# Stick-breaking attention with queries on partitions: sigmoid, product scan and transposed weights in place of matmul sums of log terms

## The reference

```python
z = jnp.einsum('bqhd,bkhd->bhqk', qb, kf) * (B_DH ** -0.5)
valid = k_pos[None, :] < qpb[:, None]
log_keep = jnp.where(valid, jax.nn.log_sigmoid(-z), 0.0)
after = lax.cumsum(log_keep, axis=3, reverse=True) - log_keep
a = jnp.where(valid, jnp.exp(jax.nn.log_sigmoid(z) + after), 0.0)
return jnp.einsum('bhqk,bkhd->bqhd', a, vf)
```

## Time and profile before

| | |
|---|---|
| time of three runs | 1991.29 us median, 1987.05 to 1993.68 |
| profiled execution, first to last instruction | 1986.7 us (0.35 us below the shortest of the three times) |
| TensorE busy, share of the span | 1859.7 us, 94% |
| VectorE | 1151.5 us, 58% |
| ScalarE | 1031.0 us, 52% |
| GpSimd | 387.6 us, 20% |
| mean granted clock of TensorE | 0.975 |
| second attention, from the first scores on | 1002.4 to 1744.8 us |
| `mix_b`, gate units of 384 rows | 1839.2 to 1923.0 us |

### The profile page before, as it was taken

One profiled execution on the slowest core, in us unless ns is written; L12 is line 12 of the kernel. 1 busy time (PEld: TensorE's weight loads), 2 busy tenths in 40 slices (PEclk: granted clock), 3 DMA queues, 4 the chain that ended last, 5 costly groups with the idle time before them and its releaser, 6 DMA issues. The chain is left out here.

```text
span 1986.7 us, 31724 instructions
## 1 busy us (share of the span) xinstructions
PE 1859.7 (94%) x11429; PEld 1615.1 (81%) x11429; DVE 1151.5 (58%) x2317; ACT 1031.0 (52%) x2452; POOL 387.6 (20%) x597
## 2 busy tenths in 40 slices
PE   4999999999999899999699999999999999899996
PEld 3888878888788779999587888888888888689995
DVE  5456465574555642355257667676767575844545
ACT  5355454564545532354256656575757575822345
POOL 0132231322313100156101010111111111200441
PEclk7999999999999999999799999999999999999999
DMA  4121112211122143221110202111112021242113
GB/s 155 45 79 38 49 49 60 65 39 49 49 60 65 44 152 90 65 73 59 60 39 22 65 28 70 38 50 39 55 33 60 28 60 49 77 135 90 54 54 127
DMA packets 161803, 125.07 MB, mean 63 GB/s; under 512 B 10992, under 2 KB 152624, under 8 KB 161648
## 3 DMA queue, kind: packets, MB, share of 16 engines
q1 hardware_dynamic: 160784, 122.85, 20.2%
q10 hardware_dynamic: 864, 0.20, 0.1%
HBM read 89.49 MB, written 33.52 MB: 62 GB/s over the span
## 5 line engine op out<-in xcount | busy, mean ns | idle before, releaser
L107 PE MATMUL pj<-h_high,area 128*128 128x384 f32 (+1 forms) x1536 | 380.4, 333 | 18.2 <-issue 5.8
L107 PE MATMUL pj<-area,h_high 128*128 128x384 f32 (+1 forms) x1152 | 333.0, 352 | 6.3 <-issue 5.5
L107 PEld LDWEIGHTS pj<-h_high,area 128*128 128x128 f32 x1536 | 271.0, 192 | 23.7 <-issue 11.1
L107 PE MATMUL pj<-h_low,area 128*128 128x384 f32 (+1 forms) x768 | 251.7, 328 | 0.0
L107 PEld LDWEIGHTS pj<-area,h_high 128*128 128x128 f32 (+1 forms) x1152 | 204.0, 181 | 18.6 <-issue 5.5
L1208 ACT ACTIVATE lb_m<-lb_sc 128x512 f32<-128x512 f32 (+4 forms) x200 | 88.5, 486 | 227.1 <-PE lb_sc L1642 196.3
L107 PE MATMUL pj<-area,h_low 128*128 128x384 f32 (+1 forms) x576 | 195.3, 339 | 0.0
L1557 POOL TENSOR_TENSOR lb_o<-lb_o,lb_keep 128x512 f32<-128x512 f32 (+3 forms) x80 | 77.6, 970 | 572.5 <-ACT lb_keep L1237 565.9
L1396 DVE SCALAR_TENSOR_TENSOR lb_s<-lb_sc,lb_m 128x512 f32<-128x512 f32 (+4 forms) x200 | 109.9, 549 | 69.0 <-ACT lb_m L1218 69.0
L107 PEld LDWEIGHTS pj<-h_low,area 128*128 128x128 f32 x768 | 147.6, 192 | 0.0
L455 ACT ACTIVATE la_p<-la_sc,la_nm 128x128 f32<-128x128 f32 (+5 forms) x144 | 105.8, 737 | 33.8 <-DVE la_nm L652 32.9
(11 more groups left out here) (310 smaller groups left out, 4394.2 us busy)
## 6 DMA issues: line engine op xcount, KB each, us to landing
stage<-in_a_w_in SPq DMA_DIRECT2D x60, 192.0 KB, 3.2
stage<-in_b_w_in SPq DMA_DIRECT2D x60, 192.0 KB, 3.2
stage<-in_ple_w_gate SPq DMA_DIRECT2D x22, 512.0 KB, 3.8
h_low<-o_t SPq DMA_DIRECT2D x14, 528.0 KB, 6.4
mix_b_xs<-x_mid SPq DMA_DIRECT2D x8, 528.0 KB
lift_xt<-in_x SPq DMA_DIRECT2D x8, 512.0 KB, 4.6
stage<-in_a_w_in SPq DMA_DIRECT2D x16, 256.0 KB, 5.0
out_ak<-la_tok SPq DMA_DIRECT2D x8, 512.0 KB, 3.3
```

The costliest lines, as they stand in the source:

```text
L107: last = pe.matmul(out, x, y, start=start and n == 0, stop=stop and n == 2, **kw)
```

## The change

`stick_layer` is turned round: queries are on partitions and keys in the free dimension. A pair is now a tile of 128 queries with up to 512 keys; tiles 4 to 7 have two pairs, the later keys first. ScalarE computes sigmoid(-z) into `remain` and sigmoid(z) into `a`, both from PSUM. VectorE turns `remain` into the running product by a scan that goes backwards over the keys, and for the earlier keys starts from the later pair's last value. GpSimd multiplies `a` by the product shifted by one key (VectorE does so for the sample). TensorE transposes the weights in blocks of 128 keys into `flip`, ScalarE copies them to `wt`, and TensorE multiplies them with the values once per 256 queries, accumulating over all key blocks in PSUM, so that the scaling by `keep` and the additions into `o` are gone. Scores banks shrink from four to three, `flip` takes two. The gate uses the sigmoid directly. `stick_layer` names the table set `sigmoid_and_others` before its first group. `diff_layer` and `mix_phase` are the same text; their lines are lower by 67 in `mix_phase`.

```diff
...
-    PAIRS = [(0, b) for b in range(4)] + [(1, 0), (2, 0)] + [(1, b) for b in range(1, 8)]
-    UNITS = [(c, b, hd) for c, b in PAIRS for hd in range(1 if c == 2 else 2)]
-    NP, N, SPLIT = len(PAIRS), len(UNITS), len(UNITS) - 1
...
+    SAMPLE_Q = NT
+    PAIRS = [(q, 0) for q in range(4)] + [(SAMPLE_Q, 0)] + [(q, c) for q in range(4, NT) for c in (1, 0)]
+    UNITS = [(q, c, hd) for q, c in PAIRS for hd in range(1 if q == SAMPLE_Q else 2)]
+    BANKS = [(0, 1), (2, 0), (1, 2), (0, 1), (1, 2)] + [(0, 1), (2, 0), (1, 2)] * 2 + [(0, 1), (2, 0)]
+    FIRST_KEY = [0, 512, 0, 512, 0] + [512, 0] * 4
+    VALUES = [0, 1, SAMPLE_Q, 2, 3]
+    NP, N = len(PAIRS), len(UNITS)
+    SAMPLE = PAIRS.index((SAMPLE_Q, 0))
+    HQ = 2 * P
...
+    value_pair = lambda v: SAMPLE if v == SAMPLE_Q else PAIRS.index((2 * v + 1, 0))
+    value_nth = lambda v: VALUES.index(v) + 1
+    VALUES_AT = {value_pair(v) + 2: v for v in VALUES}
+    width = lambda i: PAST + DEC if i == SAMPLE else min(QC, (PAIRS[i][0] + 1) * P - PAIRS[i][1] * QC)
+    diagonal = lambda i: i != SAMPLE and PAIRS[i][1] == PAIRS[i][0] // 4
+    carried = lambda i: i > SAMPLE and PAIRS[i][1] == 0
+    keys_end = lambda i: FIRST_KEY[i] + width(i) + carried(i)
...
+        remain = [sb(f"remain{i}", [P, 2 * QC]) for i in range(2)]
+        a_ = [sb(f"a{i}", [P, PAST + DEC]) for i in range(4)]
+        wt, wt_sample = [sb(f"wt{i}", [P, NT, HQ]) for i in range(2)], sb("wt_sample", [P, SB, 2 * DEC])
...
+        flip, acc, sc = pb("flip", [P, 2, 512]), pb("acc", [P, 512]), pb("sc", [P, 3, 512])
...
+                def keep(s):
                     act.wait_ge(S["z"], at.next("z"))
...
+                    act.activation(remain_of(s), scores_of(s), ACT.Sigmoid, scale=-1.0).then_inc(S["keep"], 1)
...
+                def sigmoid(s):
+
+                    act.wait_ge(S["w_turned"], at.nth("w_turned", s - 3) if s >= 4 else at.before("w_turned"))
+                    act.activation(weights_of(s), scores_of(s), ACT.Sigmoid).then_inc(S["sig"], 1)
+
+                def move(s):
+                    i, hd = pair(s), UNITS[s][2]
+                    q, c = PAIRS[i]
+                    act.wait_ge(S["w_turned"], at.nth("w_turned", s + 1))
...
+                    act.wait_ge(S["pv"], at.nth("pv", value_nth(q // 2 - 1)) if q >= 2 else at.before("pv"))
+                    nb = width(i) // P
+                    act.activation(wt[hd][:, 4 * c:4 * c + nb, q % 2 * P:(q % 2 + 1) * P],
+                                   flip[:, hd, 0:width(i)].rearrange("p (b n) -> p b n", n=P), ACT.Copy).then_inc(S["moved"], 1)
...
                 for i in range(NP + 1):
                     if i < NP:
                         for s in units(i):
-                            size(s)
-                        for s in units(i):
-                            exp(s)
-                        for s in units(i):
-                            log(s)
+                            keep(s)
+                            sigmoid(s)
                     if i >= 1:
                         for s in units(i - 1):
-                            weights(s)
-                        if PAIRS[i - 1][1] > 0:
-                            keep(i - 1)
+                            move(s)
                     if i - 1 in GATE_AT:
-                        gate_log(GATE_AT[i - 1])
-                    if i - 2 in GATE_AT:
-                        gate_sigmoid(GATE_AT[i - 2])
+                        gate_sigmoid(GATE_AT[i - 1])
...
+            act.preload_act_table_set("sigmoid_and_others")
...
+                def scan(s):
+                    i, hd = pair(s), UNITS[s][2]
+                    dve.wait_ge(S["keep"], at.next("keep"))
+                    x, first = remain_of(s)[:, ::-1], 1.0
+                    if carried(i):
+                        dve.wait_ge(S["scan"], at.nth("scan", s - 1))
+                        first = remain[hd][:, QC:QC + 1]
+                    dve.tensor_tensor_scan(out=x, data0=x, data1=x, initial=first, op0=ALU.mult, op1=ALU.min).then_inc(S["scan"], 1)
+
...
+                def take(v):
+                    dve.wait_ge(S["pv"], at.nth("pv", value_nth(v)))
...
+                    out, c = slice(v * HQ, (v + 1) * HQ), v // 2
+                    if v % 2 == 0:
...
-                add(NP - 1)
-                finish(1)
+                take(VALUES[-1])
+                dve.wait_ge(S["taken"], at.all("taken"))
...
+                def product(s):
+                    pool.wait_ge(S["scan"], at.nth("scan", s + 1))
+                    pool.wait_ge(S["sig"], at.nth("sig", s + 1))
+                    after = after_of(s)
+                    out = weights_of(s)[:, 0:after.shape[1]]
+                    pool.tensor_tensor(out, out, after, ALU.mult).then_inc(S["a"], 1)
...
+                            last = pe.matmul(scores_of(s), qt[x][f, q * P:(q + 1) * P],
+                                             kt[y][f, par, c * QC:c * QC + width(i)], start=n == 0 and not diagonal(i),
...
+                def turn_weights(i):
+                    for s in units(i):
+                        hd = UNITS[s][2]
+                        if i == SAMPLE:
+                            pe.wait_ge(S["a_sample"], at.all("a_sample"))
+                        else:
+                            pe.wait_ge(S["a"], at.nth("a", a_nth(s + 1)))
+                        pe.wait_ge(S["moved"], at.nth("moved", copied(s)) if copied(s) else at.before("moved"))
+                        x = weights_of(s)
+                        n = 2 * DEC if i == SAMPLE else P
+                        for b in range(0, width(i), P):
+                            rows = min(P, width(i) - b)
+                            last = pe.transpose(flip[0:rows, hd, b // P * n:(b // P + 1) * n], x[:, b:b + rows], ident[0:n, 0:n])
+                        last.then_inc(S["w_turned"], 1)
+
+                def values(v):
+                    i = value_pair(v)
...
+                    blocks = SB if v == SAMPLE_Q else 2 * v + 2
...
+                                q = P if b == 2 * v + 1 else 0
+                                last = pe.matmul(acc[f, q:HQ], tok_v[:, par, b, f], wt[hd][:, b, q:HQ], **kw)
...
-                    if i >= 2:
-                        values(i - 2)
+                    if i in VALUES_AT:
+                        values(VALUES_AT[i])
                     if i >= 1:
-                        for s in units(i - 1):
-                            after(s)
-                        if PAIRS[i - 1][1] > 0:
-                            column_sums(i - 1)
+                        turn_weights(i - 1)
                     if i in (0, 2, 3):
                         turn(at, i + 5)
...
-                values(NP - 1)
+                values(VALUES[-1])
...```

The places in the order of instructions that differ. First TensorE in a middle step of a group, whose pair has 512 columns (`lb_sc` scores, `lb_s` log terms, `lb_acc` values, `pj` projection). Before:

```order
L1642 MATMUL lb_sc<-lb_qk_high 128x512 x2
L1642 MATMUL lb_sc<-lb_qk_high,lb_qk_low 128x512 x2
L1642 MATMUL lb_sc<-lb_qk_low,lb_qk_high 128x512 x2
L1709 MATMUL lb_acc<-lb_a,lb_tok 64x512 x2
L1672 MATMUL lb_sc<-lb_s_high,lb_tri 128x512
L1672 MATMUL lb_sc<-lb_s_low,lb_tri 128x512
L1672 MATMUL lb_sc<-lb_s_high,lb_tri 128x512
L1672 MATMUL lb_sc<-lb_s_low,lb_tri 128x512
L1683 MATMUL lb_third<-lb_s_high,lb_half 128x512
L1683 MATMUL lb_third<-lb_s_low,lb_half 128x512
L1683 MATMUL lb_third<-lb_s_high,lb_half 128x512
L1683 MATMUL lb_third<-lb_s_low,lb_half 128x512
```

More of the change, by code:

```diff
@@ L1044, in stick_layer @@
-                     z=N, size=N, exp=N, log=N, soft=N, high=SPLIT, low=SPLIT, after=N, a=N, sums=CARRIED,
-                     keep=CARRIED, scaled=CARRIED, added=NP - 1, sampled=1, pv=NP, dve_link=4, o_ready=3,
-                     pe_tick=0, fill=1, pads=1)
+                     tok_stored=64, g_ready=3, g_normed=3, g_sig=3, g_done=3, qs_ready=1,
+                     z=N, keep=N, sig=N, scan=N, a=N - 1, a_sample=1, w_turned=N, moved=N, pv=len(VALUES), taken=len(VALUES), dve_link=0,
+                     o_ready=3, fill=1, pads=1)
@@ L1448, in finish @@
+                    ins = dve.tensor_tensor(o[:, out], acc[:, 0:HQ], gate[:, out], ALU.mult)
+                    ins.then_inc(S["taken"], 1)
                 def finish(c):
@@ L1633, in scores @@
-                        for hd in range(2):
-                            last = pe.matmul(slot[:, hd, PB * DEC:], unit[:, :], hide[:, 0:DEC], **masked)
+                        first = BANKS[i][0]
+                        for n, (x, y) in enumerate(((0, 0), (1, 0), (0, 1))):
+                            pe.matmul(sc[0:2 * DEC, first, :], qs[x][:, :], kpt[y][:, :], start=n == 0, stop=n == 2,
+                                      skip_group_check=True)
+                        new = sc[0:2 * DEC, first + 1, 0:DEC]
@@ L1635, in scores @@
+                        pe.matmul(new, hide_sample[:, :], unit[:, 0:DEC], start=True, stop=False, skip_group_check=True)
```

(23 more changed lines are left out.)

424 lines of the change are left out of this document (150 added, 274 removed).

## The result

| | before | the change |
|---|---|---|
| median | 1991.26 us | 1957.76 us |
| range, four runs each | 1987.05 to 1993.68 | 1955.77 to 1959.91 |
| profiled span | 1986.7 | 1954.0 |
| TensorE busy | 1859.7 | 1780.0 |
| VectorE, ScalarE, GpSimd busy | 1151.5, 1031.0, 387.6 | 1023.8, 976.7, 548.1 |

A forecast was written before the change was run, and what follows sets the result against it. TensorE was taken to bound the second attention, busy 721.2 of 742.4 us. The sum 1986.7 - 98 + 1 + 55 = 1944.7 us of span, with the median 4.6 above, gave 1949 us; 8 in 10 range 1922 to 1990.

The forecast's parts named there:

- the two large terms: Second attention about 97 us shorter (-98 of TensorE work, +1 of waits); table loads in mix_b +55 us.
- The work term: Second attention, TensorE: 7.5 us added, 18.5 removed, 1.3 saved by reshaping; net -12.3 a group, -98 in eight.
- with 0.10 for entering, as above, one is 0.08: Second attention: TensorE's price per 128x128 transpose, from four taking 0.42 us; 7.5 us a group in all.
- The wait term: Second attention: new waits for weights 20 us, against 19.3 going; net +1, bounds -10 and +35.
- second rival: Attention: GpSimd's product takes 1.8, not 1.30 us, slowed by VectorE's passes; 15 to 35 us more, 1964 to 1984; chance 0.15.
- hand-overs: Second attention: included in the 20 us of waits, beside about 8 us in half-piece steps and some 8 in the last group.
- None becomes the bound by volume: Second attention: ScalarE and VectorE have room; GpSimd's product comes to about 25 us a group of some 80.
- dearer switch: Rival in mix_b: a table switch costs more than its 1.28 us row; at 2.56, 2028 us, slower; chance 0.13.
- the ring: mix_b gates: units and weight splits in series over ScalarE and VectorE; 62 loads lie on it, first-pass visit 12.8 us.
- then the split up to the next unit's Exp 3.35: mix_b, first gate pass: last part of a visit's 12.8 us, read from 1950.20 to 1953.55; seven visits +16.
- The hidden loads: Third rival, mix_b: the loads stay hidden since TensorE had ScalarE idle in 51 of 83.8 us; 1894 to 1910; chance 0.05.
- The chain: Second rival, attention: scores to transposable weights, through ScalarE, VectorE and GpSimd in series, becomes the bound; 1964 to 1984; chance 0.15.

The follow-up runs named there:

- turned_twice: set_back with every transpose of weights issued twice: 1941.78 us, 45.8 us above set_back.
- head1_vector: set_back with head 1's product of weights and scan moved from GpSimd to VectorE: 1883.11 us, 12.8 below set_back.
- both_vector: set_back with both heads' products on VectorE instead of GpSimd: 1890.92 us, 5.0 below set_back.
- set_back: The changed kernel with natural_log_exp_and_others named at the start of mix_b's ScalarE stream, leaving one load there: 1895.94 us, 0.953 of before.
- before_switch: The kernel before with sigmoid_and_others named at the start of mix_b's ScalarE stream, so the same 67 loads appear: 2053.24 us, 1.031 of before.
- add_later: The changed kernel, loads kept; in mix_b GpSimd's sum for a unit waits until that unit's clamp is done: 1953.81 us, 0.981 of before.

## Why the prediction was right, point by point

**The sum.** 1949 was predicted and 1957.76 measured, 8.8 us more, on the side and inside the range. By the finer rows above, the two large terms came out as -90.0 (forecast -97) and +62.0 (forecast +55): both mechanisms as described, both sizes 7 us too kind. The 4.7 us that came back, 2.8 before the attention and 1.9 in the outputs, are no merit of the forecast: the code there is the same.

**Attention.** A middle group lasts 82.05 us (the same matmul of past keys stands at 1417.29 and 1499.34). Before, five of seven last 93.5 and two 95.0; each of the two has a short stretch at the lower clock (a mean of 0.66 from 1197 to 1202 us and 0.67 from 1571 to 1576), which no middle group has now. Like against like that is 11.4 less. The forecast had 12.3 of work and, with the earlier trace rows's 1.9 us a group gone and 1 come, some 0.9 of waits.

The work term was 0.9 too large. Counted on TensorE from start to start, the 77 transposes of this group take 8.9 us where the forecast had 7.5, and the projections 0.5 more than before; against that, the sums and the sample gave 19.5 and not 18.5. The step that was off for the transposes is "with 0.10 for entering, as above, one is 0.08": four of them still take 0.41 to the next instruction, as in the earlier trace rows, but the eight shown take 0.93 and not 0.74, and turned_twice has 0.10 each. The wait term was mis-sized as well: the group keeps 1.8 us on TensorE, as many as before, since GpSimd's product takes 1.67 and not 1.30. That was the second rival's mechanism at three quarters of its size (it took 1.8), and its claim "the two may slow each other" holds: whichever starts second pays (last section).

The waits for weights come to 22.6 us on TensorE, where the text had 20 with hand-overs. The 36.6 of the weight loads overstates the price, as head1_vector and both_vector show. "None becomes the bound by volume" held, with GpSimd's products at 33 us a group and not 25. So for a middle group the forecast was 1.8 us too kind. Part of that was made up by things that it didn't know: the first group gave 15.6, of which 2.5 are waits that only that group had, and the two slow stretches of before gave 3. That is luck.

The last group is only 3.0 us shorter than before (1581.41 to 1652.1 against 1671.20 to 1744.9), with 9.7 us of waits for products. Behind such waits the granted clock fell, too; no run here takes the waits out of this group alone, so that they caused it isn't shown. After:

```profile
1613.40:1619.40 6.00, 5.98 (x22) 4.80 (x23) 4.46 (x6) 4.01 (x8) 2.81 (x3) 0.50 0.64 262
...
1640.00:1650.40 10.40, 8.62 (x35) 5.96 (x35) 3.17 (x3) 3.15 (x6) 4.05 (x2) 0.51 0.00 0
```

At 0.50 TensorE runs at 1.2 GHz; ahead of the first row stand two waits of 1.90 and 1.43 us. Some 14.6 us of busy time at half speed are 7 us lost, which no term of the prediction held. Before, this group had a milder dip, worth 3 us:

```profile
1700.00:1710.00 10.00, 7.65 (x49) 4.95 (x48) 8.01 (x15) 9.75 (x19) 0.95 (x1) 0.79 0.97 375
1710.00:1720.00 10.00, 9.90 (x44) 6.20 (x43) 9.05 (x12) 8.73 (x16) 3.65 (x3) 0.87 0.01 4
```

**The scan** was taken at 1.1 and took 1.26, near the upper bound of 1.37. Between 128 and 512 columns it grows by (1.26 - 0.42) / 384 = 2.2 ns a column, VectorE's product in both_vector between 127 and 255 by 1.05 (0.291 and 0.425 us). The Trainium skill, "DVE: opcode table, instruction layouts, handler registers and perf-mode slots" (Datapath and trigger behaviour), says that the scan runs at half throughput; these slopes agree.

**The loads.** 67 rows of 1.28 us, as forecast, and a chance of 0.13 for a dearer switch that did not come. The load ahead of the first group fell into a wait for weights (2.3 us, before 2.1), as said. set_back and before_switch put the price at 61.8 and 62.4 us, 1.0 us for each of the 62 loads on the ring: 62 x 1.28 = 79, less the waits for VectorE that loads overlap and the slack that the first pass had. The Trainium skill, "ScalarE: Activation LUTs" (What ACT_TABLE_LOAD costs), adds 1.38 us for a drain to each load; the trace disagrees: the rows have 0.02 us ahead of and behind a load between dependent activations, and the time would have been 2035. Per part: second pass 11.33 - 6.71 = 4.6 a visit (forecast 4.5), last statistics from 9.2 to 16.9 us, 7.7 (forecast 8). The step that was mis-sized is "then the split up to the next unit's Exp 3.35": I read it in the second pass, where GpSimd is idle at that moment, and it is 4.58 in the first. That makes 13.96 for the visit and not 12.8. Over the seven visits (1750.07 to 1844.95 us, before 1844.76 to 1918.51) 21.1 us came and not 16, which is 5 of the 7 us that this term is short; the first and the last of the seven have less than the full price. add_later shows two thirds of the 1.2 in a visit to be GpSimd's sum beside VectorE's split; the rest is the split of 1024 columns (1.55 against 1.23) and the wider clamp (0.55 against 0.45).

**The rivals.** The hidden loads (1894 to 1910) and the dear switch (2028) are out. The chain is there with 22.6 us of waits on TensorE where 19.3 went, within the +35 of the range.

## What to carry to other kernels

When a stage names another table set for ScalarE, look at the order of instructions of every stage behind it: here one line cost 62 us in a stage that the change doesn't touch, and one line more at the stage's start takes the time from 1958 to 1896. A piece of a ring is to be read in the pass to which it will be applied, with the same neighbours at work; the same chain of instructions took 3.35 us in one pass and 4.58 in the other. A product handed to an idle engine costs what it takes beside the engine that feeds it (1.67 us, not 1.09). What a wait is worth is told by TensorE's own row and not by that of its weight loads: 12.4 and 21 us went from the two, and the time fell by 12.8.
